# Seventeen groups of unread products between the norms and the wide layers of a kernel of two transformer blocks

## The chip, the cores and the metric

The kernel runs on one core of a Trainium2 chip. Its engines are TensorE (PE; matrix products into the PSUM banks), VectorE (DVE), ScalarE (ACT), GpSimd (POOL) and SyncE (SP, which here only issues loads). They run side by side and wait for each other through semaphores. The metric is the time of one execution on the device, in microseconds, as the median of several runs; less is better.

## The reference

Two blocks are computed for 512 tokens of width 1024. The first has two layers: one with a latent attention of 8 heads, which also carries 256 context tokens (768 together), and one with a gated linear attention of 4 heads; each is followed by a norm, a residual, a norm with modulation and an MLP with squared ReLU. The second has a gated delta rule of 8 heads and a retention of 4 heads, each followed by a layer norm, and by a convolutional feed-forward layer with another one. Cut to what matters here:

```
def rms_norm(x, g):
    y = x * rsqrt(mean(x * x, axis=-1) + NORM_EPS);  return y * g
h = modulate(rms_norm(x, norm_g[i, 0]), m[0], m[1])
y = mla_mixer(h, ...) if i == 0 else gla_mixer(h, ...)
x = x + m[2] * rms_norm(y, norm_g[i, 1])
h = modulate(rms_norm(x, norm_g[i, 2]), m[3], m[4])
x = x + m[5] * rms_norm(square(relu(h @ w1)) @ w2, norm_g[i, 3])
...
y = mixers[i](x * (1 + sc1) + sh1)             # delta rule, retention
x = layer_norm(ALPHA * x + (1 + g1) * y)
y = conv_ffn(x * (1 + sc2) + sh2)
x = layer_norm(ALPHA * x + (1 + g2) * y)
```

## The kernel before, in words

The residual stream lies transposed in `xT`: 8 blocks of 128 features by 768 or 512 tokens. A norm needs the sum of squares over features, that is, over partitions. ScalarE squares block after block into one of two buffers `sq` (L1301), and TensorE adds the blocks up by multiplying with a square of ones (`square_sum`, records L674 and L677, into the bank `sc[:, 0]`). When the last block is in, ScalarE takes a logarithm and an exponential (L1308, L1310, with a table load ahead of each), VectorE multiplies all blocks with the result (L1722 or L1738), adds the residual (L1742, L1743), and ScalarE modulates (L1325 to L1343). In all that time TensorE has nothing to do until the next squares or inputs come.

Wide products (output projections, MLPs, feed-forward layers, retention inputs) are computed from numbers split in two: a high part that ScalarE copies (`w_hi`, `x_hi`, `x_lo` as the high part of an output projection) and the rest, which VectorE subtracts (`w_lo`, `x_lo`, `attn_lo`, `g_out_lo`, `d_out_lo`, `wide_lo`; L1899, L1920, L1926, L1929). Three products of the halves stand for one; each leaves one record in the trace. All other f32 products leave two. In the first pass over an input TensorE waits for each of the 8 (or 16) blocks to be split; the later passes need no such wait.

Products go to the bank pairs `acc` and `sc`. The bank `sc[:, 1, 0]` takes scores, a projection and the sums of the linear attention at other times, and the bank beside it, `sc[:, 1, 1]`, collects the modulation (L735). `base_tab` holds an identity and the square of ones, side by side, 256 columns.

The order on each engine is that of the program text; an engine starts an instruction when its semaphores are there. No scheduler moves anything. The loops run over heads, quarters of the MLP width and column groups; the norms stand between them, outside of any loop.

Of the kernel before, what the change touches and what calls it, by code (L numbers as in the profile page):

```python
# [12 lines left out]
P = 128  # L13
# [10 lines left out]
GLA_H, GLA_DV, GATE_RANK = 4, 256, 16  # L24
# [110 lines left out]
def first_and_second_block(nc, A, out):  # L135
    ctx = ExitStack()
    with ctx:
        def sb(name, shape, dt=F32):
            return ctx.enter_context(nc.sbuf_tensor(name, shape, dt))

        def sem(name):
            return ctx.enter_context(nc.semaphore(name))
# [11 lines left out]
        base_tab = sb("base_tab", [P, 2 * P])  # L154
        ident, ones = base_tab[:, 0:P], base_tab[:, P:2 * P]
# [41 lines left out]
        sc = ctx.enter_context(nc.psum_tensor("sc", [P, 2, 2, 512], F32))  # L197
# [167 lines left out]
        gr_ready, gss_ready, gdev_ready = sem("gr_ready"), sem("gss_ready"), sem("gdev_ready")  # L365
# [73 lines left out]
        def emptied(eng, stage, it, j):  # L439

            u = UNIT0[stage] + j
            eng.wait_ge(acc_free[u % 2], u // 2 + 1 + it * (UNITS[stage] // 2))
# [190 lines left out]
        def _(pe):  # L633
# [32 lines left out]
            def square_sum(name, n, blocks=None):  # L666

                _, b0, nb = NORMS[name]
                for b in blocks or range(nb):
                    pe.wait_ge(n_sq, b0 + b + 1)  # L670
                    s = sq[:, (b0 + b) % 2]
                    if n == T:
                        for h in range(2):
                            last = pe.matmul(sc[:, 0, h, 0:HALF], ones, s[:, h * HALF:(h + 1) * HALF],  # L674
                                             start=b == 0, stop=b == nb - 1)
                    else:
                        last = pe.matmul(sc[:, 0, 0, 0:n], ones, s[:, 0:n], start=b == 0, stop=b == nb - 1)  # L677
                    last.then_inc(n_used, 1)

            def mean_sum(stage):  # L680

                for b in range(DB):
                    emptied(pe, stage, *divmod(b, UNITS[stage]))
                    last = pe.matmul(sc[:, 0, 1, :], ones, xT[:, b, CTX:T], start=b == 0, stop=b == DB - 1)  # L684
                last.then_inc(n_mean, 1)
# [65 lines left out]
            for h in range(2):  # L751
                last = pe.matmul(unit("mla_rope", 0)[:, h, 0:HALF], dup, kraw[0:64, h * HALF:(h + 1) * HALF],
                                 start=True, stop=True)
# [2 lines left out]
            pe.matmul(unit("mla_rope", 1)[:, 0, :], rotdup, kraw[0:64, CTX:T], start=True,  # L756
                      stop=True).then_inc(acc_ready, 1)
            square_sum("cq", T)
            square_sum("ckv", T)
            pe.wait_ge(lat_ready, 5)  # L760
            pe.wait_ge(krope_ready, 2)
            S = "mla_pair"
            columns = [None]
            with pe.Fori(0, MLA_H // 2) as it:
# [22 lines left out]
                for j in range(2):  # L787
                    claim(pe, S, it, 8 + j)
                    pe.matmul(unit(S, 8 + j)[:, 0, 0:256], rot2, qraw[:, CTX + 256 * j:CTX + 256 * (j + 1)],
                              start=True, stop=True).then_inc(acc_ready, 1)  # L790
# [49 lines left out]
            def second_half(stage, it, j):  # L840
                pe.wait_ge(w_split, half_group(stage, it, j, 1))
# [9 lines left out]
            def out_proj(stage, nk, per, squares=None):  # L851

                for j in range(8):
                    if squares and j > 2:
                        square_sum(*squares, [j - 3])
                    if j % per == 0:
                        w = split_group(stage, 0, j // per, nk, per * P)
                    claim(pe, stage, 0, j)
                    for k in range(nk):
                        if j == 0:  # L860
                            pe.wait_ge(o_split, OUT0[stage] + k + 1)
                        if j % per == 0 and k == nk // 2:
                            second_half(stage, 0, j // per)
                        last = split_product(unit(stage, j), w, (j % per) * P, k, out_parts(stage, k), k == 0, k == nk - 1)
                    last.then_inc(acc_ready, 1)
                if squares:
                    square_sum(*squares, range(5, 8))

            out_proj("mla_out", DB, 2, ("y0", T))

            def input_split(k, before):
# [3 lines left out]
            def mlp(i, n):  # L875
                S = f"mlp{i}"
                if n == T:
                    spans = [(h, HALF, slice(h * HALF, (h + 1) * HALF)) for h in range(2)]
                else:
                    spans = [(0, n, slice(0, n))]  # L880
                with pe.Fori(0, 4) as it:
                    for u in range(16):
                        if u % 2 == 0:
                            w = split_group(S, it, u // 2, DB, 256)
                        claim(pe, S, it, u)
                        for k in range(DB):
                            if u == 0:
                                input_split(k, DB * i)
                            if u % 2 == 0 and k == DB // 2:
                                second_half(S, it, u // 2)  # L890
                            if u == 8:
                                pe.wait_ge(relu_free, it * DB + (4 * DB * i + k + 3))
                            x = x_parts(n, k) if u < 8 else [(h, w_, hid_hi[:, k, t], hid_lo[:, k, t]) for h, w_, t in spans]
                            last = split_product(unit(S, u), w, (u % 2) * P, k, x, k == 0, k == DB - 1)
                        last.then_inc(acc_ready, 1)
                        if u in MOD_SUM_AFTER:
                            mod_sum(i, it, MOD_SUM_AFTER[u], 2 - i)

            square_sum("h0m", T)
            pe.wait_ge(mod_ready, 2)  # L900
            mlp(0, T)
            square_sum("y0m", T)


            square_sum("h1", T)
            pe.wait_ge(gate1_in, 16 * 2)
            for d in range(2):
                claim(pe, "gla_gate", 0, d)
# [4 lines left out]
            with pe.Fori(0, GLA_H) as it:  # L913
# [76 lines left out]
                for b in range(2):  # L990
                    last = pe.matmul(sc[:, 1, 0, :], ones, sq[:, b, 0:SEQ], start=b == 0, stop=b == 1)
                last.then_inc(gss_ready, 1)
            out_proj("gla_out", DB, 2, ("y1", SEQ))
            square_sum("h1m", SEQ)
            mlp(1, SEQ)
            square_sum("y1m", SEQ)


            pe.wait_ge(ab_in, 48)
# [18 lines left out]
            for r in range(2):  # L1018
                for c in range(LT):
# [5 lines left out]
                      stop=True).then_inc(d_cols, 1)  # L1025
# [131 lines left out]
            with pe.Fori(0, GDN_H // 2 - 1) as it:  # L1157
                gdn_pair(it, False)
            gdn_pair(GDN_H // 2 - 1, True)
            out_proj("gdn_out", DB, 2)  # L1160

            def ffn(i):
# [32 lines left out]

            mean_sum("gdn_out")
            square_sum("ln0", SEQ)
            ffn(0)
            mean_sum("ffn0_down")
            square_sum("ln0f", SEQ)  # L1200


            S = "ret_head"
            with pe.Fori(0, RET_H) as it:
# [62 lines left out]
                for b in range(4):  # L1267
                    pe.wait_ge(r_sq, it * 4 + b + 1)
                    last = pe.matmul(unit(S, 11)[:, 0, :], ones, r_sqr[:, b, :], start=b == 0, stop=b == 3)
                last.then_inc(acc_ready, 1)  # L1270
            out_proj("ret_out", 2 * DB, 1)
            mean_sum("ret_out")
            square_sum("ln1", SEQ)
            ffn(1)
            mean_sum("ffn1_down")
            square_sum("ln1f", SEQ)

            pe.wait_ge(x_ready, 64)
            for t in range(LT):
# [1203 lines left out]
```

## Time and profile before

| | us |
|---|---|
| median of 3 runs | 4133.73 (4129.1 to 4134.78) |
| the profiled execution, its own time | 4134.98 |
| its span, first to last instruction | 4133.3 |
| TensorE busy in it | 3758.0 (91%) |
| VectorE busy | 1793.3 (43%) |
| ScalarE busy | 1228.4 (30%) |
| mean granted clock of TensorE, as a share of full speed | 0.956 |

Times in the profile count from the start of the span. A record's duration is not its cost in a stream: products are pipelined, and their starts stand closer than they are long. What a product costs behind another is read from a stretch with many of them, divided by their number. The granted clock is 1.00 at 2.4 GHz and 0.50 at 1.2 GHz; a mean between them tells how much of a stretch lay at either level. The idle time in square brackets at the end of a row is that of the engine just ahead of the row, with the instruction that ended it.

### The profile page before, as it was taken

Reading aid. Unit: us, or ns where it says so; the run is one execution under the profiler, and the core shown is the slowest. Engines: PE = TensorE matmul, PEld = TensorE weight load, DVE = VectorE, ACT = ScalarE, POOL = GpSimd, SP = SyncE. Lnnn points to the kernel's source line nnn. Section 1 sums busy time; section 2 is a strip of 40 time slices with the busy share of each in tenths; the row PEclk is TensorE's granted clock in tenths of the full one; section 3 lists DMA queues with packets and bytes.
Section 4 is the critical chain, followed back from the end, with each engine's and each line's share of the span. In section 5 each row is a group of like instructions: output and inputs, shape, how many; then the busy total and the mean of one; then the engine's idle time right before and its main releaser. Section 6 shows DMA issues by size and latency. Waiting matters only on the chain.

```text
span 4133.3 us, 45599 instructions
## 1 busy us (share of the span) xinstructions
PE 3758.0 (91%) x17410; PEld 2905.1 (70%) x17410; DVE 1793.3 (43%) x2580; ACT 1228.4 (30%) x1511; POOL 155.9 (4%) x292
## 2 busy tenths in 40 slices
PE   6899997999998989799989999799977899899998
PEld 3477786999994656488856555668856677677876
DVE  1244445454444333455535544544444433435433
ACT  2111125132224222433323333244411322235432
POOL 0000000010000000011100000000022000000000
PEclk9999999999998999899999999899988999999999
DMA  4021112333220011144421011022255211122222
GB/s 153 31 83 62 62 54 69 103 120 100 94 91 31 31 36 36 57 164 165 162 90 31 31 41 33 18 79 91 91 167 171 87 61 61 61 82 88 95 86 76
DMA packets 300088, 335.15 MB, mean 81 GB/s; under 512 B 12113, under 2 KB 266449, under 8 KB 299857
## 3 DMA queue, kind: packets, MB, share of 16 engines
q1 hardware_dynamic: 271456, 250.69, 18.9%
q0 software_dynamic: 23040, 75.52, 5.5%
q10 hardware_dynamic: 5489, 7.47, 0.5%
q8 instruction: 76, 1.25, 0.1%
q14 instruction: 27, 0.22, 0.0%
HBM read 331.55 MB, written 2.10 MB: 81 GB/s over the span
## 4 chain that ended last, share of the span: by engine, by line
PE 83%; DVE 5%; ACT 4%; DMA 3%; issue 3%; ACTq 1%; DVEq 0%; POOLq 0%; POOL 0%; SPq 0%
PE acc L643 60%; PE sc L643 4%; PE sc L1086 2%; PE sc L674 2%; PE acc L823 1%; PE sc L797 1%; PE sc L799 1%; DMA rows_or_mod<-in_ada_w 1%; PE sc L735 1%; DMA rstd<-in_ada_w 1%; PE acc L1086 1%; PE sc L677 1%; PE acc L1256 1%; PE sc L684 1%; ACTq L1366 1%
## 5 line engine op out<-in xcount | busy, mean ns | idle before, releaser
L643 PE MATMUL acc<-x_lo,w_hi 128*128 128x512 f32 (+1 forms) x2048 | 775.8, 379 | 35.5 <-DVE d_out_lo L1899 10.5
L1417 ACT ACTIVATE w_hi<-wring 128x1024 fp32r<-128x1024 f32 (+1 forms) x368 | 352.0, 1004 | 1031.3 <-DMA wring<-in_mlp_w 479.6
L1920 DVE TENSOR_TENSOR w_lo<-wring,w_hi 128x1024 fp32r<-128x1024 f32 (+1 forms) x368 | 412.7, 1163 | 531.9 <-ACT w_hi L1417 531.7
L643 PEld LDWEIGHTS acc<-x_lo,w_hi 128*128 128x128 f32 x2048 | 388.8, 190 | 98.8 <-DVE w_lo L1920 28.4
L643 PE MATMUL acc<-hid_hi,w_hi 128*128 128x512 f32 (+1 forms) x1120 | 417.4, 373 | 5.1 <-DVE w_lo L1920 4.9
L643 PE MATMUL acc<-hid_hi,w_lo 128*128 128x512 f32 (+1 forms) x1120 | 413.0, 369 | 0.0
L643 PE MATMUL acc<-x_hi_holes,w_hi 128*128 128x512 f32 x704 | 279.1, 396 | 14.8 <-DVE x_lo L1926 14.8
L643 PE MATMUL acc<-x_hi_holes,w_lo 128*128 128x512 f32 x704 | 278.5, 396 | 0.0
L643 PE MATMUL acc<-hT,wring 128*128 128x512 f32 (+2 forms) x640 | 260.0, 567 | 14.1 <-DVE arena L1993 12.0
L643 PE MATMUL acc<-hid_lo,w_hi 128*128 128x384 f32 (+1 forms) x768 | 270.8, 353 | 0.0
L643 PE MATMUL acc<-x_hi_seq,w_hi 128*128 128x512 f32 x576 | 229.0, 398 | 14.4 <-DVE x_lo L1929 14.4
L643 PEld LDWEIGHTS acc<-hid_hi,w_hi 128*128 128x128 f32 x1120 | 214.5, 191 | 32.5 <-DVE w_lo L1920 6.9
L643 PEld LDWEIGHTS acc<-hid_hi,w_lo 128*128 128x128 f32 x1120 | 213.4, 191 | 25.3
L643 PEld LDWEIGHTS acc<-hT,wring 128*128 128x128 f32 (+1 forms) x640 | 124.8, 197 | 147.7 <-issue 97.0
L643 PE MATMUL acc<-x_hi_seq,w_lo 128*128 128x512 f32 x576 | 225.7, 392 | 0.0
L628 POOL DMA_DIRECT2D rows_or_mod<-in_ada_w x192 | 104.0, 542 | 2811.9 <-DVE hT L1722 1243.1
L643 PE MATMUL acc<-wide_lo,w_hi 128*128 128x512 f32 x480 | 192.6, 401 | 0.0
L1799 DVE SCALAR_TENSOR_TENSOR tab<-rows_or_mod,cs,tab 128x512 f32<-128x512 f32 x224 | 163.0, 748 | 61.6 <-DMA rows_or_mod<-in_ada_w 56.3
L643 PE MATMUL acc<-x_hi,w_hi 128*128 128x384 f32 x512 | 173.6, 339 | 13.5 <-DVE x_lo L1929 11.0
L643 PE MATMUL acc<-x_hi,w_lo 128*128 128x384 f32 x512 | 172.2, 336 | 2.1 <-issue 2.1
L643 PE MATMUL sc<-hT,wring 128*128 128x512 f32 x384 | 172.8, 595 | 0.4 <-DVE d_col L2100 0.4
L643 PEld LDWEIGHTS acc<-x_hi_holes,w_hi 128*128 128x128 f32 x704 | 133.0, 189 | 51.6 <-issue 14.8
(373 smaller groups left out, 5910.3 us busy)
## 6 DMA issues: line engine op xcount, KB each, us to landing
wring<-in_mlp_w SPq DMA_DIRECT2D x64, 1024.0 KB, 5.5
rows_or_mod<-in_ada_w POOLq DMA_DIRECT2D x192, 256.0 KB, 3.2
wring<-in_ffn_up SPq DMA_DIRECT2D x44, 1024.0 KB, 5.0
wring<-in_ada_w SPq DMA_DIRECT2D x12, 2048.0 KB, 7.8
rstd<-in_ada_w POOLq DMA_DIRECT2D x96, 256.0 KB, 3.2
wring<-in_ret_w_in SPq DMA_DIRECT2D x24, 1024.0 KB, 5.2
wring<-in_ffn_down SPq DMA_DIRECT2D x32, 704.0 KB, 4.6
wring<-in_gdn_w_in SPq DMA_DIRECT2D x16, 1024.0 KB, 5.7
```

What stands on the lines that cost most here:

```text
L628: pool.dma_start(mod_w[p % MOD_SLOTS], w[:, k, bass.ds(it * (MOD_IT * MOD_N) + i * MOD_N, MOD_N)]).then_inc(mod_loaded[p % MOD_SLOTS], 16)
L643: ins = pe.matmul(o, lhsT, rhs, start=start, stop=stop)
L674: last = pe.matmul(sc[:, 0, h, 0:HALF], ones, s[:, h * HALF:(h + 1) * HALF], start=b == 0, stop=b == nb - 1)
L677: last = pe.matmul(sc[:, 0, 0, 0:n], ones, s[:, 0:n], start=b == 0, stop=b == nb - 1)
L684: last = pe.matmul(sc[:, 0, 1, :], ones, xT[:, b, CTX:T], start=b == 0, stop=b == DB - 1)
L735: last = pe.matmul(mod_psum[:, bass.ds(it * (MOD_IT * per * nv) + c, 1)], mod_acc[:, i % 2, v, m * P:(m + 1) * P], ones[:, 0:1], start=Tru ...
L797: pe.matmul(sc[:, n % 2, h, 0:w], qn[:, e, t * P:(t + 1) * P], kn[:, e, k0:k0 + w], start=True, stop=False)
L799: last = pe.matmul(sc[:, n % 2, h, 0:w], qr[:, t * P:(t + 1) * P], krope[:, e, k0:k0 + w], start=False, stop=True)
L1086: last = pe.matmul(o[:, e, t], left[:, e, t], right[:, e, t], start=True, stop=True)
L1417: f(w_hi[s][:, c], wring[s][:, c], ACT.Copy).then_inc(w_high, 1)
L1799: ins = stt(a, mod_w[s], cs[:, k, v:v + 1], a, MUL, ADD)
L1920: tt(w_lo[s][:, c], wring[s][:, c], w_hi[s][:, c].bitcast(F32), SUB).then_inc(w_split, 1)
```

## The change

A new function on TensorE's side issues a number of products, 256 columns each, of the square of ones with the whole of `base_tab`, into `sc[:, 1, 0]`. Nothing reads that bank between such products and the next real product into it. The number is the argument divided by 0.43, rounded down. It is called at seventeen points of the program, all outside of loops; at one of them (ahead of the linear attention's output projection) a wait is added, for the last exponential of that attention, `gdev_ready`, because ScalarE has read a sum from this bank shortly before. No other engine's program is changed.

```
+            def keep_running(us):
+                for _ in range(int(us / 0.43)):
+                    pe.matmul(sc[:, 1, 0, 0:2 * P], ones, base_tab[:, :], start=True, stop=True)
...
             square_sum("cq", T)
+            keep_running(3)
             square_sum("ckv", T)
+            keep_running(6)
             pe.wait_ge(lat_ready, 5)
...
+            keep_running(6)
             out_proj("mla_out", DB, 2, ("y0", T))
...
+            keep_running(11.5)
             square_sum("h0m", T)
+            keep_running(6.5)
             pe.wait_ge(mod_ready, 2)
             mlp(0, T)
             square_sum("y0m", T)
+            keep_running(12.5)
             square_sum("h1", T)
+            keep_running(5)
             pe.wait_ge(gate1_in, 16 * 2)
...
+            pe.wait_ge(gdev_ready, GLA_H)
+            keep_running(7)
             out_proj("gla_out", DB, 2, ("y1", SEQ))
+            keep_running(8.5)
             square_sum("h1m", SEQ)
+            keep_running(5)
             mlp(1, SEQ)
             square_sum("y1m", SEQ)
+            keep_running(10)
             pe.wait_ge(ab_in, 48)
...
+            keep_running(9.5)
             out_proj("gdn_out", DB, 2)
...
             square_sum("ln0", SEQ)
+            keep_running(5)
             ffn(0)
             mean_sum("ffn0_down")
             square_sum("ln0f", SEQ)
+            keep_running(5)
...
+            keep_running(8)
             out_proj("ret_out", 2 * DB, 1)
             mean_sum("ret_out")
             square_sum("ln1", SEQ)
+            keep_running(5)
             ffn(1)
             mean_sum("ffn1_down")
             square_sum("ln1f", SEQ)
+            keep_running(8)
             pe.wait_ge(x_ready, 64)
```

TensorE's order ahead of the attention, before: sums of `cq` and `ckv` squares stand in one row, behind the key products.

```order
L643 MATMUL acc<-hT,wring 64x384 x16
L752 MATMUL acc<-arena,tab 128x384 x2
L756 MATMUL acc<-arena,tab 128x512
L674 MATMUL sc<-sq,base_tab 128x384 x10
L764 UNCONDITIONAL_BRANCH
```

The same place in the changed kernel, where the code's lines from L683 on are new or shifted (L674 is the sum, L683 the new product).

```order
L643 MATMUL acc<-hT,wring 64x384 x16
L757 MATMUL acc<-arena,tab 128x384 x2
L761 MATMUL acc<-arena,tab 128x512
L674 MATMUL sc<-sq,base_tab 128x384 x6
L683 MATMUL sc<-base_tab 128x256 x6
L674 MATMUL sc<-sq,base_tab 128x384 x4
L683 MATMUL sc<-base_tab 128x256 x13
L771 UNCONDITIONAL_BRANCH
```

Six products now stand between the two sums and thirteen behind the second; the sums themselves keep their order.

TensorE's order at the end of the linear attention with its waits, before: the last sum of squares (L991), the loop's end, and the output projection.

```order
L991 MATMUL sc<-sq,base_tab 128x512 [waits gsq_ready]
L991 MATMUL sc<-sq,base_tab 128x512
L913 REGISTER_ALU
L913 COMPARE_AND_BRANCH
L643 MATMUL acc<-x_lo,w_hi 128x512 [waits o_split,acc_free0,w_split]
L643 MATMUL acc<-g_out_lo,w_hi 128x512
```

The same place in the changed kernel.

```order
L1003 MATMUL sc<-sq,base_tab 128x512 [waits gsq_ready]
L1003 MATMUL sc<-sq,base_tab 128x512
L925 REGISTER_ALU
L925 COMPARE_AND_BRANCH
L683 MATMUL sc<-base_tab 128x256 [waits gdev_ready]
L683 MATMUL sc<-base_tab 128x256 x15
L643 MATMUL acc<-x_lo,w_hi 128x512 [waits o_split,acc_free0,w_split]
L643 MATMUL acc<-g_out_lo,w_hi 128x512
```

The new wait stands between the loop and the sixteen products; the projection keeps its own waits.

## Rows read from the trace of the kernel before

**Rows 1.** Page: busy share and instructions; clock in 40 slices; the chain by engine

```profile
PE 3758.0 (91%) x17410; PEld 2905.1 (70%) x17410; DVE 1793.3 (43%) x2580; ACT 1228.4 (30%) x1511; POOL 155.9 (4%) x292
...
PEclk9999999999998999899999999899988999999999
...
PE 83%; DVE 5%; ACT 4%; DMA 3%; issue 3%; ACTq 1%; DVEq 0%; POOLq 0%; POOL 0%; SPq 0%
```

**Rows 2.** Timeline, TensorE: start, us, engine, line, tiles, shapes, count [idle before <-releaser]

```profile
160.84 4.50 PE L674 MATMUL sc<-sq,base_tab 128*128 128x384 f32 x8 [3.88 <-ACT sq L1301]
...
651.07 12.88 PE L674 MATMUL sc<-sq,base_tab 128*128 128x384 f32 x32 [12.28 <-ACT sq L1301]
...
1239.23 10.48 PE L674 MATMUL sc<-sq,base_tab 128*128 128x384 f32 x32
1263.40 12.21 PE L674 MATMUL sc<-sq,base_tab 128*128 128x384 f32 x32 [13.69 <-ACT sq L1301]
1281.24 23.73 PE L643 MATMUL acc<-hT,gate 128*16 128x384 f32 x64 [5.63 <-ACT hT L1327]
```

**Rows 3.** Stretches behind restarts: us, busy PE PEld DVE ACT POOL, PEclk, DMA, GB/s

```profile
172.08:179.08 7.00, 7.00 (x13) 3.95 (x14) 0.00 (x0) 0.00 (x0) 0.00 (x0) 0.59 0.26 75
559.98:566.98 7.00, 7.00 (x31) 7.00 (x32) 5.93 (x7) 4.38 (x7) 0.00 (x0) 0.74 0.44 150
1669.13:1676.13 7.00, 7.00 (x23) 5.66 (x24) 4.07 (x7) 2.99 (x6) 0.00 (x0) 0.73 0.47 150
1731.22:1738.22 7.00, 7.00 (x12) 2.54 (x12) 6.20 (x7) 3.76 (x6) 0.00 (x0) 0.78 0.00 0
2129.84:2136.84 7.00, 7.00 (x12) 1.26 (x13) 3.59 (x6) 6.17 (x9) 0.00 (x0) 0.72 0.00 0
2676.71:2683.71 7.00, 7.00 (x24) 5.61 (x25) 4.06 (x8) 3.06 (x6) 0.00 (x0) 0.78 0.45 152
3615.51:3622.51 7.00, 7.00 (x25) 5.71 (x26) 7.00 (x13) 7.00 (x15) 0.00 (x0) 0.79 0.53 150
```

**Rows 4.** The same view, a stretch of 96 records of 256 columns and two neighbours

```profile
1329.70:1350.42 20.72, 20.72 (x98) 18.19 (x97) 11.67 (x23) 4.08 (x6) 0.00 (x0) 1.00 0.15 51
```

**Rows 5.** Timeline, TensorE: the first row behind nine other bubbles

```profile
172.08 7.30 PE L643 MATMUL acc<-arena,wring 128*128 128x384 f32 x13 [6.75 <-DVE arena L1833]
...
559.98 0.66 PE L643 MATMUL acc<-x_lo,w_hi 128*128 128x384 f32 x1 [6.42 <-DVE attn_lo L1899]
...
1669.13 0.77 PE L643 MATMUL acc<-x_lo,w_hi 128*128 128x512 f32 x1 [9.73 <-DVE g_out_lo L1899]
...
1731.22 1.22 PE L677 MATMUL sc<-sq,base_tab 128*128 128x512 f32 x1 [9.20 <-ACT sq L1301]
...
2129.84 15.79 PE L643 MATMUL acc<-hT,w_ab 128*8 128x512 f32 x32 [10.85 <-ACT hT L1336]
...
2676.71 0.76 PE L643 MATMUL acc<-x_lo,w_hi 128*128 128x512 f32 x1 [10.46 <-DVE d_out_lo L1899]
...
2744.86 0.76 PE L643 MATMUL acc<-x_hi_holes,w_hi 128*128 128x512 f32 x1 [5.93 <-DVE x_lo L1926]
...
3615.51 0.77 PE L643 MATMUL acc<-x_lo,w_hi 128*128 128x512 f32 x1 [8.85 <-DVE wide_lo L1899]
...
4122.69 0.69 PE L1283 MATMUL sc<-base_tab,xT 128*128 128x128 f32 x2 [9.33 <-ACT xT L1351]
```

**Rows 6.** Timeline, VectorE behind the sum at 651.07, and ScalarE ahead of 1669.13

```profile
667.07 1.83 DVE L1722 TENSOR_TENSOR hT<-xT,rstd 128x768 f32<-128x768 f32 x2 [0.90 <-ACT rstd L1310]
...
1661.44 0.63 ACT L1525 ACTIVATE rstd<-rstd 128x512 f32<-128x512 f32 x1
```

**Rows 7.** Stretches as in rows 3: two first passes of wide layers

```profile
676.20:685.87 9.67, 6.19 (x29) 4.58 (x29) 6.69 (x9) 9.54 (x15) 1.74 (x3) 1.00 0.31 106
2744.86:2754.35 9.49, 7.66 (x21) 4.26 (x21) 7.72 (x13) 9.28 (x14) 1.61 (x3) 0.83 0.48 159
```

**Rows 8.** Stretches as in rows 3: the last transposes and their four copies

```profile
4122.69:4130.04 7.35, 6.05 (x32) 5.56 (x32) 4.80 (x4) 0.00 (x0) 0.00 (x0) 0.70 0.39 156
```

More of the change, by code:

```diff
@@ L678, in square_sum, with keep_running @@
                     last.then_inc(n_used, 1)
+            def keep_running(us):
+                for _ in range(int(us / 0.43)):
+                    pe.matmul(sc[:, 1, 0, 0:2 * P], ones, base_tab[:, :], start=True, stop=True)
             def mean_sum(stage):
@@ L758, in _ @@
             square_sum("cq", T)
+            keep_running(3)
             square_sum("ckv", T)
+            keep_running(6)
             pe.wait_ge(lat_ready, 5)
@@ L867, in out_proj @@
                     square_sum(*squares, range(5, 8))
+            keep_running(6)
             out_proj("mla_out", DB, 2, ("y0", T))
@@ L897, in mlp @@
                             mod_sum(i, it, MOD_SUM_AFTER[u], 2 - i)
+            keep_running(11.5)
             square_sum("h0m", T)
+            keep_running(6.5)
             pe.wait_ge(mod_ready, 2)
@@ L902, in _ @@
             square_sum("y0m", T)
+            keep_running(12.5)
             square_sum("h1", T)
+            keep_running(5)
             pe.wait_ge(gate1_in, 16 * 2)
@@ L992, in _ @@
                 last.then_inc(gss_ready, 1)
+            pe.wait_ge(gdev_ready, GLA_H)
+            keep_running(7)
             out_proj("gla_out", DB, 2, ("y1", SEQ))
+            keep_running(8.5)
             square_sum("h1m", SEQ)
+            keep_running(5)
             mlp(1, SEQ)
             square_sum("y1m", SEQ)
+            keep_running(10)
             pe.wait_ge(ab_in, 48)
@@ L1159, in _ @@
             gdn_pair(GDN_H // 2 - 1, True)
+            keep_running(9.5)
             out_proj("gdn_out", DB, 2)
@@ L1197, in _ @@
             square_sum("ln0", SEQ)
+            keep_running(5)
             ffn(0)
@@ L1200, in _ @@
             square_sum("ln0f", SEQ)
+            keep_running(5)
             S = "ret_head"
@@ L1270, in _ @@
                 last.then_inc(acc_ready, 1)
+            keep_running(8)
             out_proj("ret_out", 2 * DB, 1)
@@ L1273, in _ @@
             square_sum("ln1", SEQ)
+            keep_running(5)
             ffn(1)
@@ L1276, in _ @@
             square_sum("ln1f", SEQ)
+            keep_running(8)
             pe.wait_ge(x_ready, 64)
```

## Prediction, before the changed kernel had run

> **What bounds the kernel now.** I read the page first. TensorE is busy 91% of the span and holds 83% of the chain that ended last, and the line of its granted clock is full nearly everywhere but dips to 8 in five of forty slices [rows 1]. So time is to be had where TensorE stands or runs at its lower level (1.2 instead of 2.4 GHz). Second, the timeline of TensorE around the places that the diff names: each row shows how long the engine stood, who let it go, and how long the work took that followed. Before the sum of squares at 1263.40 it stood 13.69 us, and the 32 records of that sum then took 12.21 us; the same 32 records at 1239.23, straight behind other products, took 10.48 [rows 2]. Third, the table by stretch: in the 7 us behind such an idle the granted clock averages 0.59 to 0.78 while TensorE is busy all 7 us [rows 3]. The kernel pays twice for a bubble: the bubble, which ScalarE and VectorE set, and slow products behind it.
>
> **What the change adds.** Seventeen calls issue 273 products (6, 13, 13, 26, 15, 29, 11, 16, 19, 11, 23, 22, 11, 11, 18, 11, 18), and one wait. Nothing is removed or moved. A plain f32 product leaves two records; 96 records of 256 columns follow each other in the 20.72 us of [rows 4] at full clock, 0.216 us each, so a product costs 0.432 us and all of them 118 us. They cost nothing as long as they end before the producer behind the next wait does. I check that bubble by bubble, product count times 0.432 against the idle: 2.6 of 3.88, 11.2 of 12.28, 12.5 of 13.69, 4.8 of 5.63 [rows 2]; 5.6 of 6.75, 5.6 of 6.42, 8.2 of 9.20, 9.9 of 10.85, 9.5 of 10.46, 7.8 of 8.85, 7.8 of 9.33, 4.8 of 5.93 [rows 5]. Four more calls stand in bubbles like the last one, ahead of the first pass of a wide layer. What is left of each bubble is 0.8 to 1.6 us, so I expect no late restart there, at full clock. The cover is the chain of logarithm, exponential, multiplications and splits on ScalarE and VectorE, which doesn't depend on these products: nobody reads the bank. If that chain were 1 us quicker in a bubble, its products would cost that excess.
>
> **What it gives, place by place.** If the clock stays at 2.4 GHz through the bubble, work that ran at half speed behind it takes half of that stretch. That is a gain only where TensorE itself then sets the pace.
> - Second norm of the attention (160.84): 8 records took 4.50 us; at 10.48/32 each they take 2.6. They follow each other without a break, so TensorE sets the pace: 1.8 us after rounding [rows 2].
> - First attention products (172.08), seven whole us at a clock of 0.59: 7 x 0.41 = 2.9 us. By the same product: the attention's output projection (559.98) 1.8, the sum at 1731.22 1.5, the gate products at 2129.84 2.0, the output projections at 2676.71 and 3615.51 1.5 each [rows 3]. In the projections VectorE has to keep ahead: at 559.98 a split takes 0.85 us (5.93 for 7), and 31 records in 7 - 1.8 us of full-clock work are 0.168 each, 1.0 for the six of a block; at 2676.71 it is 0.5 against 0.68 for three [rows 3]. So the products stay the slower side.
> - The sum at 1263.40: 12.21 - 10.48 = 1.7. The gate products at 1281.24: 64 records, 23.73 - 64 x 0.3275 = 2.8 us [rows 2].
> - The sum at 651.07: 12.88 - 10.48 = 2.4 on TensorE, but then VectorE starts the next multiplications at 667.07 after only 0.90 us of idle behind weight splits [rows 6]. VectorE is late next, so 0.9.
> - The linear attention's output projection (1669.13). Here the products wait for an exponential that ends at 1662.07 [rows 6], so that the bank has been read. Behind that wait stand only these products and the projection, whose own wait ends later. TensorE has then stood 2.7 us (since 1659.40), and 16 products end at 1669.0, with 0.1 us to spare. If the clock has fallen by then they overrun, by at most half of the slow stretches seen behind restarts (2.9 to 5.7 us, from 14 x (1 - clock)), so by up to 2.9. Full gain 7 x 0.27 = 1.9 [rows 3]; bounds -0.9 and 1.9. The idle lies between 3.88, behind which the products were slow, and the short pieces that left the clock full [rows 7]; it is near to neither, so I take the middle of the bounds, 0.5.
> - The last transposes (4122.69): 7.35 x 0.30 = 2.2 at most, but VectorE's four copies fill 4.80 of those 7.35 us and follow the first quarter of the transposes [rows 8]. I take 1.5.
> - The first passes of both MLPs, both convolution layers and the retention heads (five calls): nothing. There ScalarE is busy 9.54 of 9.67 and 9.28 of 9.49 us while TensorE waits for each block [rows 7]; when its last block comes, a full clock has only waited longer. For the same reason an overrun of a us or two costs nothing either.
>
> Sum: 1.8 + 2.9 + 1.8 + 1.5 + 2.0 + 3.0 + 1.7 + 2.8 + 0.9 + 0.5 + 1.5 = 20.4 us. The profiled execution took 4134.98 us, 1.7 more than its span, which the products don't touch; that gives 4114.6. The three timed runs had a median of 4133.73, 1.3 lower, which gives 4113.3. I forecast **4113 us**. How long the clock stays low behind a restart varies from place to place (2.9 to 5.7 us), and so does how often it falls in the loops that the change leaves alone; the three runs spread over 5.7 us.
>
> **Rivals.**
> *The clock falls anyway.* What is left of the bubbles, 0.8 to 1.6 us, may be enough to lose the clock, above all where the engine then works in pieces. Then the products buy nothing and the time is 4134, or 4130 with a few places won. Against it: between 676.20 and 685.87 TensorE was busy only 6.19 of 9.67 us, in pieces, and its clock was 1.00 throughout [rows 7]. The Trainium skill (TensorE: Matmul & The Clock Gate, section "A second HAM failure mode: psum-queue depth-cycling") says that frequent micro-idles between groups of matmuls make the clock swing between its levels. By that rule this rival would be the forecast; in this stretch the trace does not agree. I give it 9%.
> *Other engines set the restarts.* If the splits or squares, and not TensorE, pace the sums and projections as they do the first passes, only the attention's first products, the two gate products and the small norm pay in full: 2.9 + 2.0 + 2.8 + 1.8 = 9.5 us, with a little from the rest 12, so 4122. For it: it holds at five of seventeen places. Against it: in the sums TensorE's records leave no idle, and at full clock they took 10.48 without any. 12%.
> *The products are late (slower).* They are sized for 2.4 GHz. If a constant times ones doesn't keep the clock up, each takes 0.86 us and the bubble's products end long behind the producer. At the twelve places that pay (at the other five a late start is absorbed) they take 92 us at full clock; at half of it 92 us more, less some 12 us of slack, is 80 us: 4214. If the clock rises after at most 5.7 slow us, each loses at most 2.9, is 1.9 us late and then runs at full clock: 12 x 1.9 - 21 = +2, 4136. It is slower than 4142 from 2.4 us of lateness at each of the twelve. Against it: the sums multiply by the same ones and kept the clock for 10.48 us at 1239.23, and nearly all calls follow directly on such full-clock work [rows 2]. 4%.
> *The change doesn't do what it says.* If a product took half of 0.432 us, half of each bubble would stay empty and the clock fall; no gain, 4133. Against it are the 96 records of [rows 4]. 3%.
>
> **How the numbers follow.** Forecast 70%: 4113, give or take 6 for its bounds (the doubtful projection ±1.4, the transposes ±0.7, the varying slow stretches some ±3, the loops left alone ±3). Other engines 12%: 4122. Clock falls anyway 9%: 4132. Late products 4%: above 4142. No effect 3%: 4133. The rest, 2%, is more gain than summed, down to 4100. The range must reach the second case: 4104 to 4125. A measurement of this kernel can tell some 0.2%, 8.3 us, from no change: the bounds are 4125.5 and 4142. Faster: 70 + 12 + 2 = 84%, same 9 + 3 = 12%, slower 4%.
>
> **What would show it.** In the profile of the changed kernel each of the seventeen bubbles should hold the new line's records 0.216 us apart, with the idle before the restart down to 0.8 to 1.6 us (none at 1669). The granted clock behind the twelve paying restarts should be 1.00, and the sums of 32 records at 10.5 us. The first passes should end no earlier relative to their norm. The forecast is wrong if records stand 0.43 us apart, if restarts wait for no producer but for the products, if the clock behind them is still near 0.7, or if VectorE or ScalarE idles less than before yet TensorE's waits grow by as much as its products shrink.

## The result, and the profile of the changed kernel

The changed kernel took 4114.41 us (median of six runs, 4110.44 to 4116.82) beside 4134.18 for the kernel before (median of six): a ratio of 0.9950, 95% interval 0.9936 to 0.9964, some 20 us less. The forecast was 4113, range 4104 to 4125. The profiled execution took 4116.82 us with a span of 4115.1 (before: 4133.3).

The page, answering [rows 1]: busy share and instructions of each engine, the granted clock in 40 slices, the chain by engine.

```profile
PE 3852.5 (94%) x17956; PEld 2995.1 (73%) x17956; DVE 1792.6 (44%) x2580; ACT 1228.1 (30%) x1511; POOL 155.5 (4%) x292
...
PEclk9999999999999999999999999999988999999999
...
PE 82%; DVE 5%; ACT 4%; DMA 4%; issue 3%; ACTq 1%; DVEq 0%; POOLq 0%; POOL 0%; SPq 0%
```

TensorE is busy 94.5 us longer and yet ends 18 us earlier, since 118 us of products were added. VectorE, ScalarE and GpSimd do what they did. Three of the five dips in the line of the clock are gone; the two left lie in the second half of the first convolution layer, which the change leaves alone.

The timeline of TensorE at bubbles, answering [rows 2] and [rows 5] (line 683 is the new product; lines behind it have moved by up to 23):

```profile
152.64 2.75 PE L683 MATMUL sc<-base_tab 128*128 128x256 f32 x12
156.69 2.85 PE L674 MATMUL sc<-sq,base_tab 128*128 128x384 f32 x8 [1.29 <-ACT sq L1324]
159.37 5.78 PE L683 MATMUL sc<-base_tab 128*128 128x256 f32 x26
166.28 10.08 PE L643 MATMUL acc<-arena,wring 128*128 128x384 f32 x30 [1.14 <-DVE arena L1856]
...
632.79 11.39 PE L683 MATMUL sc<-base_tab 128*128 128x256 f32 x52
645.23 10.59 PE L674 MATMUL sc<-sq,base_tab 128*128 128x384 f32 x32 [1.06 <-ACT sq L1324]
...
1238.07 12.68 PE L683 MATMUL sc<-base_tab 128*128 128x256 f32 x58
1251.93 10.59 PE L674 MATMUL sc<-sq,base_tab 128*128 128x384 f32 x32 [1.18 <-ACT sq L1324]
...
1268.14 20.80 PE L643 MATMUL acc<-hT,gate 128*16 128x384 f32 x64 [0.88 <-ACT hT L1350]
...
1644.82 8.86 PE L683 MATMUL sc<-base_tab 128*128 128x256 f32 x32 [2.72 <-ACT rstd L1548]
1653.33 0.58 PE L643 MATMUL acc<-x_lo,w_hi 128*128 128x512 f32 x1
```

The 13.69 us ahead of the sum of 32 records [rows 2] are now 58 records in 12.68 us and 1.18 us of idle, and the sum takes 10.59 us instead of 12.21. Who lets TensorE go at these places is the same as before: results of ScalarE (squares, modulation) and of VectorE (splits above all). The one exception is the linear attention's output projection, which starts straight behind the last product, with no idle.

The same 7 us as in [rows 3] and the last transposes of [rows 8] (columns as there), for the attention's first products, the attention's output projection, the linear attention's, the sum that answers 1731.22, the gate products, the output projections of the gated delta rule and of the retention, and the last transposes:

```profile
166.28:173.28 7.00, 7.00 (x22) 4.22 (x23) 0.96 (x1) 0.00 (x0) 0.00 (x0) 1.00 0.24 75
555.81:562.81 7.00, 7.00 (x40) 7.00 (x41) 5.93 (x7) 3.41 (x5) 0.00 (x0) 1.00 0.47 152
1653.33:1660.33 7.00, 7.00 (x32) 5.80 (x31) 2.70 (x6) 1.70 (x3) 0.00 (x0) 1.00 0.45 150
1713.78:1720.78 7.00, 7.00 (x15) 2.46 (x16) 6.20 (x7) 4.85 (x8) 0.00 (x0) 1.00 0.00 0
2116.31:2123.31 7.00, 7.00 (x17) 1.51 (x18) 3.58 (x6) 6.17 (x9) 0.00 (x0) 1.00 0.00 0
2659.47:2666.47 7.00, 7.00 (x30) 5.71 (x31) 4.07 (x7) 2.86 (x5) 0.00 (x0) 1.00 0.46 152
3598.38:3605.38 7.00, 7.00 (x31) 5.82 (x32) 7.00 (x13) 7.00 (x15) 0.00 (x0) 1.00 0.53 150
4105.82:4110.45 4.63, 4.15 (x32) 3.43 (x32) 3.45 (x3) 0.00 (x0) 0.00 (x0) 1.00 0.31 123
```

The clock column reads 1.00 in every row (2.4 GHz) where it read 0.59 to 0.79, and the count of products in the 7 us has gone from 13 to 22, from 31 to 40, from 23 to 32. VectorE's busy time in the output projection at 555.81 is the same 5.93 us: the splits kept ahead.

### The profile page after: what moved, and what is told of

It reads as the page before. It is cut to its first block, busy times and chain, and to the rows that moved or that the text cites. A ratio compares the mean times of both kernels' runs of the same rounds, so it can differ in the third digit from the quotient of the medians.

```text
span 4115.1 us, 46691 instructions
## 1 busy us (share of the span) xinstructions
PE 3852.5 (94%) x17956; PEld 2995.1 (73%) x17956; DVE 1792.6 (44%) x2580; ACT 1228.1 (30%) x1511; POOL 155.5 (4%) x292
## 4 chain that ended last, share of the span: by engine, by line
PE 82%; DVE 5%; ACT 4%; DMA 4%; issue 3%; ACTq 1%; DVEq 0%; POOLq 0%; POOL 0%; SPq 0%
PE acc L643 59%; PE sc L643 4%; PE sc L1103 2%; PE acc L830 1%; PE sc L804 1%; PE sc L806 1%; PE sc L674 1%; DMA rows_or_mod<-in_ada_w 1%; PE sc L740 1%; DMA rstd<-in_ada_w 1%; PE acc L1103 1%; DMA wring<-in_mlp_w 1%; PE sc L677 1%; PE acc L1276 1%; PE sc L689 1%
## 5 line engine op out<-in xcount | busy, mean ns | idle before, releaser
L1943 DVE TENSOR_TENSOR w_lo<-wring,w_hi 128x1024 fp32r<-128x1024 f32 (+1 forms) x368 | 412.5, 1162 | 536.7 <-ACT w_hi L1440 536.7
```

The lines of the kernel that those rows point to most:

```text
L1943: tt(w_lo[s][:, c], wring[s][:, c], w_hi[s][:, c].bitcast(F32), SUB).then_inc(w_split, 1)
```

## The experiments

Theory: behind each bubble at which TensorE sets the pace, half of the stretch at the lower clock is won, and only there. Rivals: the gain has another source (a new layout of the program, other places); any work in the bubble would do; the five first passes pay as well. The runs below were made in three sets; a kernel's ratio is to the kernel before in its own set.

**The twelve paying calls alone.** Of the seventeen, the five calls ahead of first passes go:

```diff
-            keep_running(6.5)
             pe.wait_ge(mod_ready, 2)
             mlp(0, T)
...
-            keep_running(5)
             mlp(1, SEQ)
```

and the same ahead of `ffn(0)`, the retention heads and `ffn(1)`.

> The five calls ahead of the first passes of the two MLPs, the two convolution layers and the retention heads are left out, the other twelve stay. Theory (a full clock pays only where TensorE sets the pace): the five give nothing, so the time stays at that of the whole change, 4114 us, give or take 3, and the first passes end as long behind their norm as with the calls. Rival (a fuller clock pays at every restart): each of the five was worth 1 to 2 us like the others, so 4119 to 4124.

Measured: 4117.24 us, ratio to before 0.9948 (0.9932 to 0.9963); the whole change in the same set of runs 4115.4, 0.9944 (0.9929 to 0.9959). The 2 us between them can't be told from nothing, but not surely from the rival's 5 either; the trace decides. In the first convolution layer's first pass, which runs over the 8 blocks that VectorE splits, the timeline of TensorE shows the first and the last block's restart, and the table by stretch the pass between them (columns as in [rows 3]). Without the call:

```profile
2726.52 0.77 PE L643 MATMUL acc<-x_hi_holes,w_hi 128*128 128x512 f32 x1 [5.93 <-DVE x_lo L1944]
...
2736.01 0.50 PE L643 MATMUL acc<-x_hi_holes,w_hi 128*128 128x512 f32 x1 [0.39 <-DVE x_lo L1944]
```

```profile
2726.52:2736.01 9.49, 8.22 (x22) 4.74 (x22) 7.72 (x13) 9.28 (x14) 1.61 (x3) 0.74 0.50 154
```

In the changed kernel, with it:

```profile
2726.19 0.47 PE L643 MATMUL acc<-x_hi_holes,w_hi 128*128 128x512 f32 x1 [1.18 <-DVE x_lo L1949]
...
2735.68 0.50 PE L643 MATMUL acc<-x_hi_holes,w_hi 128*128 128x512 f32 x1 [0.41 <-DVE x_lo L1949]
```

```profile
2726.19:2735.68 9.49, 6.68 (x21) 3.37 (x21) 7.72 (x13) 9.28 (x14) 1.61 (x3) 1.00 0.50 159
```

The pass takes 9.49 us at a clock of 0.74 as at 1.00: VectorE's splits set it. At the second MLP, the retention heads and the second convolution layer it is the same, with 0.59 to 0.79 without the call and 1.00 with it in the first 7 us. The first MLP can say nothing on a full clock. Its bubble is longer, its call left 2.32 us of idle, and the clock fell in spite of it:

```profile
664.61:671.61 7.00, 6.31 (x21) 5.39 (x22) 6.20 (x7) 6.87 (x11) 0.00 (x0) 0.58 0.49 150
```

So four calls are worth nothing because another engine sets the pace, and the fifth did not keep the clock.

**The same instructions, with nothing in them.**

```diff
-                    pe.matmul(sc[:, 1, 0, 0:2 * P], ones, base_tab[:, :], start=True, stop=True)
+                    pe.matmul(sc[:, 1, 0, 0:2], ones, base_tab[:, 0:2], start=True, stop=True)
```

> All 17 calls stay with their 273 products, but each product has 2 columns instead of 256, so that the bubbles are nearly as empty as before while the program holds the same instructions. Theory (the gain is the clock, held by the streaming of columns): the clock falls as before and the time is that of before, 4134 us, give or take 4; the twelve restarts show a granted clock of 0.6 to 0.8 in the 7 us behind them. Rival (the gain is another layout of the instructions: with the change the five or six idles of 0.5 to 1 us at the loop turns of the first MLP, 4.6 us in all, were gone): those idles are gone here too, 4129. Rival (any product keeps the clock up): 4114, clock 1.00 behind the restarts.

Measured: 4136.73 us, 0.9994 (0.9986 to 1.0003): no gain that these runs can tell. The changed kernel, which has the same instructions with 256 columns each, took 4115.4 us in the same set, 21 us less, so the gain doesn't come from the layout of the program. The timeline ahead of the sum of 32 records, and the table by stretch for part of that bubble, of this kernel:

```profile
1244.77 9.44 PE L683 MATMUL sc<-base_tab 128*128 128x2 f32 x56
1258.48 11.99 PE L674 MATMUL sc<-sq,base_tab 128*128 128x384 f32 x32 [4.28 <-ACT sq L1324]
```

```profile
1247.70:1254.20 6.50, 6.50 (x31) 6.42 (x31) 4.87 (x6) 1.51 (x2) 0.00 (x0) 0.50 0.25 81
```

TensorE counts as busy for all of these 6.5 us, and the granted clock is 0.50 all the same: busy time in the table does not tell whether the clock will hold. The idles at the loop turns of the first MLP were gone here too: it took 561.6 us from its first products to the next sum of squares, instead of 567.8 and 567.4 in the two profiles of the kernel before. So that rival holds for those idles, 6 us in the trace (in the time of the whole 2 us show, with an interval from 6 less to 1 more), but not for the 21 us.

**Half the products.** The divisor in `keep_running` is doubled, so the second half of each bubble stays empty.

```diff
-                for _ in range(int(us / 0.43)):
+                for _ in range(int(us / 0.86)):
```

> Each of the 17 calls issues half of its products (132 in all), so the second half of each bubble is empty: idles of about 2.6 us ahead of the attention's second norm, 3.3 to 4.2 us at the gate products of the linear attention and in the attention, and 5 to 7.5 us at most others. Theory (what counts is how long TensorE stands just ahead of the restart; in the kernel before a restart behind 3.88 us was slow already): most restarts are slow again, two or three are not, 4129 us (4124 to 4134). Rival (some work inside the bubble is enough, wherever it stands): the clock stays full, 4114 us.

Measured: 4133.58 us, 0.9988 (0.9976 to 1.0000). Of the twelve places eleven were slow again (0.59 to 0.80 in the 7 us behind the restart), the shortest behind 2.59 us of idle, so nearly all the gain was gone; two or three were expected to hold. The one that held is the linear attention's output projection. Its timeline here:

```profile
1657.00 5.41 PE L683 MATMUL sc<-base_tab 128*128 128x256 f32 x16 [2.72 <-ACT rstd L1548]
1664.01 0.47 PE L643 MATMUL acc<-x_lo,w_hi 128*128 128x512 f32 x1 [1.61 <-DVE g_out_lo L1922]
```

Eight products, run partly at the lower clock, ended 1.6 us ahead of the restart, and from the sum of squares to the end of that projection it took 60.88 us; the whole change, with 16 late products, took 62.48, and the kernel before 62.62.

**One and a half times the products.**

```diff
-                for _ in range(int(us / 0.43)):
+                for _ in range(int(1.5 * us / 0.43)):
```

> All 17 calls with one and a half times their products (409 instead of 273). Theory (at the twelve paying places TensorE sets the pace, and what a call overruns comes onto the time; at the five first passes it is absorbed): half of each call's length less the idle that the changed kernel has left there, 0 + 1.7 + 2.0 + 4.5 + 5.0 + 1.5 + 3.5 + 3.1 + 4.0 + 3.8 + 2.8 + 2.3 = 34 us, so 4148 us (4143 to 4155), with a full clock behind all restarts. Rival (the restarts are set by other engines, the gain has come from elsewhere): 4114 to 4125.

Measured: 4149.3 us, 1.0033 (1.0020 to 1.0046), 35 us above the changed kernel (34 to 37 by the ratios of the two sets) for 34 summed. At none of the seventeen places does the restart now wait for a producer, as here around the sum of 32 records:

```profile
1252.11 18.73 PE L683 MATMUL sc<-base_tab 128*128 128x256 f32 x86
1270.67 10.48 PE L674 MATMUL sc<-sq,base_tab 128*128 128x384 f32 x32
1280.99 7.50 PE L683 MATMUL sc<-base_tab 128*128 128x256 f32 x34
```

So the length is what the gain hangs on in both directions: short and the clock is lost, long and the excess is paid in full.

**The doubtful projection, with the wait removed.** Another bank needs no wait for the exponential:

```diff
-            pe.wait_ge(gdev_ready, GLA_H)
-            keep_running(7)
+            keep_running(9, 1)
...
-                    pe.matmul(sc[:, 1, 0, 0:2 * P], ones, base_tab[:, :], start=True, stop=True)
+                    pe.matmul(sc[:, 1, h, 0:2 * P], ones, base_tab[:, :], start=True, stop=True)
```

> Ahead of the linear attention's output projection the products go into the other bank of the same pair, so that they need no wait for the exponential, and there are 20 of them instead of 16. Theory (there the clock fell in the idle ahead of the products, 16 of them then ran late and ate the gain): they now follow the last head's sum directly, the clock stays full, about 1 us of idle is left, and this place gives 1.6 us more: 4112.8 us, a step that only the trace can tell from 4114.4. Rival (the projection is paced by its splits there): the same time as the whole change, with more idle inside the projection.

```profile
1638.13 8.88 PE L683 MATMUL sc<-base_tab 128*128 128x256 f32 x40
1648.08 0.47 PE L643 MATMUL acc<-x_lo,w_hi 128*128 128x512 f32 x1 [1.06 <-DVE g_out_lo L1921]
```

From the sum to the projection's end 60.86 us instead of 62.48: 1.62 won, as expected. The time, 4115.98 us (0.9947, 0.9935 to 0.9959), can't show so little.

**The two kernels once more,** unaltered.

> The changed kernel once more, unaltered, for a second profile: 4114 us, give or take 3. If the idles at the loop turns of the first MLP are a matter of the program, they are absent again, and the waits of the second MLP for late weight splits (4.4 us in the first profile) are there again; if they are a matter of the single execution, one of the two differs.

> The kernel before, unaltered, for a second profile: 4134 us (4128 to 4140). If the idles of 0.5 to 1 us at the loop turns of the first MLP and the lack of late weight splits in the second MLP are a matter of the program, both are here again as in its first profile; if they are a matter of the single execution, one of the two differs.

Measured: 4115.4 and 4137.65 us. Waits of TensorE in the first MLP's loop (line, what it waited for: us in total, times, longest), kernel before, first and second profile:

```profile
PE acc L643 <- issue: 4.6, 6, 1.1
```

```profile
PE acc L643 <- issue: 4.1, 6, 1.0
```

Neither profile of the changed kernel has such a row: a matter of the program. In the second MLP it is the other way. The first profile of before had none of the waits below, the second has them, and so has the changed kernel; first before (second profile), then changed:

```profile
PE acc L643 <- DVE arena L1955: 3.7, 3, 2.1
```

```profile
PE acc L643 <- DVE arena L1978: 4.4, 5, 2.1
```

From that MLP's start to the gate products behind it, it took 383.5 us in the first profile of before, 388.4 in the second, 388.9 in the changed kernel and 387.0 to 392.6 in the nine others. That this place seemed to lose 5.4 us was the luck of one execution of the kernel before.

**Into the loops.** What is left at the lower clock lies in loops. The first version put 3 products ahead of each sum and 7 behind the gate products of a linear-attention head, 8 between the two sums of squares of a delta-rule pair, 2 at the scores of an attention pair.

```diff
+                keep_running(1.3, 1)
                 pe.wait_ge(gsq_ready, it * 1 + 1)
...
+                    if j == 2:
+                        pe.wait_ge(qk_moved, it * 2 + 2)
+                        keep_running(3.5, 1)
                     pe.wait_ge(d_sq, it * 3 + n)
```

> The version before this one, and such products also inside three loops: 2 ahead of the first scores of each pair of attention heads, 3 ahead of the sum and 7 behind the gate products of each head of the linear attention, 8 between the two sums of squares of each pair of heads of the gated delta rule. Theory (a clock that fell in a bubble costs half of its low stretch wherever TensorE sets the pace): per head of the linear attention 10 us at the lower clock go, 5 us gained, times 5, less an overrun or two; per pair of the gated delta rule up to 17 us of it, 8 us gained in two of four; per pair of attention heads 1.7; together 25 to 40 us, so 4082 us (4072 to 4095). Rival (inside the loops VectorE and ScalarE set the pace, as at the five first passes): 4113 us, with the idles longer by what the products save.

Measured: 4103.13 us, 0.9923 (0.9910 to 0.9935): some 11 us less than the changed kernel, where 25 to 40 were expected: outside the stated range, and not the rival's 4113 either. A head of the linear attention and two pairs of the delta rule, changed kernel and then this one (columns as in [rows 3]):

```profile
1464.15:1553.17 89.02, 80.50 (x316) 53.60 (x315) 30.38 (x47) 24.11 (x29) 0.00 (x0) 0.92 0.11 36
2302.06:2554.70 252.64, 233.96 (x1113) 150.95 (x1112) 129.51 (x225) 79.67 (x96) 0.00 (x0) 0.95 0.11 33
```

```profile
1464.22:1550.60 86.38, 83.07 (x336) 57.31 (x335) 30.39 (x47) 24.11 (x29) 0.00 (x0) 0.96 0.12 37
2295.12:2542.68 247.56, 234.73 (x1144) 155.18 (x1145) 129.50 (x225) 79.42 (x97) 0.00 (x0) 0.98 0.12 34
```

A head gained 2.6 us where 5 were expected, a pair 2.5. The clock still fell twice in that head. The first fall lay on the 7 products behind the gate products, and so they took 4.98 us instead of some 3.0 (14 records at 0.216) and ended late, with no idle behind them:

```profile
1466.99 4.98 PE L683 MATMUL sc<-base_tab 128*128 128x256 f32 x14
```

The second, from 1522.1 to 1525.6, lay among the state products. In the attention's loop I had put the products behind the wait and not ahead of it: they filled nothing, and that part tells nothing.

The second version has none there, 8 products at the end of a head instead of 7 behind the next one's gate products, and 3 and 1 more among the state products.

```diff
+                        if (d, i) in ((0, 4), (1, 0)):
+                            keep_running(1.3 if d == 0 else 0.43, 1)
...
                 last.then_inc(gss_ready, 1)
+                keep_running(3.5, 1)
```

> The version with products inside the loops, rearranged after its trace: none in the attention's loop, where the first version gained nothing; per head of the linear attention 8 behind the sum of squares (ahead of the next head's gate products, and not behind them, so that the first head has none), 3 ahead of that sum and 3 and 1 ahead of the two later groups of state products, where the clock fell; per pair of the gated delta rule 2 and 8 ahead of the two sums. In the first version a head took 87.2 and 86.4 us instead of 89.1, a pair 123.4 instead of 125.6. Theory (the clock that is left low in those loops still costs TensorE half of its stretch where it sets the pace): heads of 85 to 86 us and pairs of 122 to 123, 4098 us (4090 to 4104). Rival (other engines set what is left): 4103 us as the first version, its idles longer instead.

Measured: 4093.61 us, 0.9895 (0.9880 to 0.9910), faster than both kernels, about 20 us below the changed one. The same stretches:

```profile
1454.92:1540.72 85.80, 83.61 (x345) 57.47 (x344) 30.37 (x49) 24.11 (x29) 0.00 (x0) 0.98 0.12 37
2281.62:2527.52 245.90, 234.78 (x1153) 156.31 (x1153) 129.47 (x225) 79.43 (x97) 0.00 (x0) 0.99 0.12 34
```

The whole loop of heads took 370.6 us from the gate products to the output projection, after 385.2 in the changed kernel and 379.1 in the first version; the delta rule 534.6 after 543.2 and 536.7.

**Where another engine sets the pace.** In the first convolution layer's second half TensorE waits for the modulation:

```diff
+                                if j == 0:
+                                    keep_running(5.2)
                                 mod_sum(2, it, DOWN_SUM_AFTER[j, k], 1)
...
+                            keep_running(5.2)
                             mod_sum(2, it, 2, 1)
```

> The whole change, and 12 products (5.2 us) ahead of each of the eight sums of the modulation in the first convolution layer's second half at which TensorE stands 5.8 to 9.7 us, and behind which its clock is low for some 10 us. Theory (there VectorE's chain of modulation products sets when TensorE goes on, 64.6 us of waits in all; a full clock behind such a sum only lengthens the next wait): no gain, 4114 us (4109 to 4118), waits on VectorE at those sums longer in total than the 64.6 us less the products. Rival (TensorE sets the pace behind each restart): 8 stretches of 10 us at half speed, 5 us each, 40 us less: 4075 us.

Measured: 4109.32 us, 0.9928 (0.9908 to 0.9949), which can't be told from the changed kernel; the 40 us of the rival are excluded. Waits of TensorE there, changed kernel and then this one:

```profile
PE sc L740 <- DVE tab L1822: 64.6, 8, 9.7
```

```profile
PE sc L740 <- DVE tab L1825: 23.8, 8, 4.2
```

The stretch's clock, from the first of those waits to the layer's end:

```profile
2984.96:3206.42 221.46, 156.81 (x607) 123.79 (x607) 100.15 (x146) 22.62 (x30) 50.34 (x93) 0.81 0.52 161
```

```profile
2982.59:3199.30 216.71, 192.10 (x799) 154.88 (x799) 100.42 (x146) 22.63 (x30) 50.22 (x93) 0.91 0.53 164
```

Waits plus products (8 times 5.2) are 65.3 us, as before 64.6: the products went into the waits. The clock rose from 0.81 to 0.91, and the stretch became 4.7 us shorter in this trace, not the 22 (0.10 of 221) that it would give if TensorE set its length. The 4.7 us are more than the spread between executions, since the same stretch took 219.9 to 222.4 us in the eleven other profiles. So most of the products' effect went into the waits, as the theory has it, but its "no gain" was off by some 3 to 5 us.

## Why the prediction was right

**The places.** What each gave, as the growth of the distance between the two traces (before and changed kernel, first profiles) across the place, beside the forecast:

| Place | gave, us | forecast |
|---|---|---|
| second norm of the attention | 1.66 | 1.8 |
| first attention products | 2.84 | 2.9 |
| attention's output projection | 1.68 | 1.8 |
| sum answering 651.07, up to the MLP's start | 0.99 | 0.9 |
| sum answering 1263.40 | 1.63 | 1.7 |
| gate products, linear attention | 2.93 | 2.8 |
| linear attention's output projection | 0.14 | 0.5 |
| sum answering 1731.22 | 1.51 | 1.5 |
| gate products, delta rule | 1.9 | 2.0 |
| output projections, delta rule and retention | 1.43 + 1.40 | 3.0 |
| last transposes | 1.45 | 1.5 |
| four of the five first passes | 0 | 0 |
| first pass of the first MLP | -1.5 | 0 |

The twelve paying places give 19.6 together for 20.4. The forecasts were read from the same profile of the kernel before. Against its second profile they also give 20, but single places differ by up to 1.6: the gate products of the linear attention give 1.4 there, those of the delta rule 2.9. So the total is firmer than its terms. What was read off ahead held at eleven paying places: half of the stretch at the lower clock, 0.8 to 1.6 us of idle left, VectorE as the next limit at the MLP's start. There the sum itself became 2.29 us shorter (10.59 instead of 12.88) and the MLP started only 0.99 earlier relative to it; the rest stands as idle.

**The one term that was mis-sized** is the linear attention's output projection, 0.14 for 0.5 of bounds -0.9 and 1.9. Both halves of its mechanism are in the trace: behind the 2.72 us of idle the products began at a clock of 1.00, which fell to 0.50 from 1645.4 to 1648.8, so that they took 8.86 us instead of 6.9 and the restart came 11.23 us behind the sum instead of 9.73, and the projection then ran 1.65 us shorter at full clock. The run with another bank and the run with half the products show that the late part can be had back.

**One reading was loose:** "Four more calls stand in bubbles like the last one" is wrong for the first MLP. Its bubble was 7.5 us, and the 1.3 us that the sum ahead of it gained without the MLP starting earlier made it 8.8, for 6.5 us of products; the prediction had counted that rest as lost, but not as idle here. So 2.3 us were left and the clock fell. The call could save nothing by it: the pass took as long without it (665.12 to 679.55 from the first block to the last, 664.61 to 679.03 with it). In the first profile of the changed kernel the clock fell once more, at 679.4, when the last block had come and TensorE set the pace; that is the 1.5 us in the table. The run without the five calls shows the same fall, the second profile of the changed kernel does not.

**The rivals.** *The clock falls anyway* fell at the paying places: 1.00 behind eleven of eleven idles of 0.8 to 1.6 us, while in the run with half the products idles from 2.6 us up lost it. It came true in the first MLP's first pass, where the engine works in pieces: in the changed kernel the clock was low from 665.8 to 672.6 and from 679.4 to 682.8, with idles of 0.7 to 0.8 us between. So the row of the same pass at 1.00 [rows 7], on which the prediction leant against this rival, did not carry over. The Trainium skill (TensorE: Matmul & The Clock Gate, section "A second HAM failure mode: psum-queue depth-cycling") ties swings of the clock to frequent micro-idles; the fall at 679.4 agrees. No such swing shows behind the paying restarts, nor in the four other first passes, whose idles were 0.3 to 0.5 us. *Other engines set the restarts* holds for the first passes, as forecast; the run without their calls shows it at four of the five. *The products are late* was put to the test by longer ones, and its price (half of each call less the idle left) came out as 35 us for 34 summed. *It doesn't do what it says* fell with 52 records in 11.39 us.

**What the sum left out** has terms as large as a quarter of it, and came out nearly even: the two spans differ by 18.2 us where the places gave 19.6. The first MLP gave 4.6: some 6 from the idles at its loop turns, which had nothing to do with the clock, less the 1.5 of its first pass. The start gave 4.2, the loops of the linear attention and the delta rule 1.3 and 1.8 (in the first, the last sum itself became 1.7 us slower, because a fall of the clock now lay on it). The attention's loop took 4.5 (7 falls of the clock in it instead of 3), the second MLP 5.4, the two convolution layers 1.6 each. The repeated profiles place the first MLP's idles in the program, and the second MLP, the start and the attention's loop in the execution (in the second profile of the changed kernel the start gave nothing, the attention's loop 1.7); which falls in the loops come with a given execution was not settled. So the forecast's error of 1 us is partly luck; the 6 us that it allowed itself were nearer to what it could know. The comparison that is free of the idles, with the kernel of 2 columns, gives 21 us for 20.4.

## What to carry to other kernels

Products that nobody reads are worth issuing where three things hold: the engine stands long enough to lose the clock, it sets the pace behind the restart, and they fit the bubble (0.8 to 1.6 us left kept the clock at eleven places, 2.3 lost it at one). Read each of the three from the trace of that place, not from shares of the whole: here twelve of seventeen places paid, 1.6 us on average, one of them next to nothing. A loop pays per turn, so look there next, and put the products ahead of the wait, in a bank that needs no wait of its own.

## What the runs showed of the hardware that was not expected

**The clock fell while the engine was busy.** In the run with 2 columns, TensorE followed one record with the next from 1244.63 to 1254.20 without idle, and from 1247.70 on the granted clock was 0.50 (the row is with that run); with 58 records of 256 columns in the same place it was 1.00 throughout.

**Instructions added in one place removed idles in another.** The kernel before stands 4.1 and 4.6 us in two profiles, in six pieces of up to 1.1 us, at the loop turns of the first MLP. With the 273 products, full or of two columns, there are none; without the five calls, or with half or one and a half times the products, three pieces and 2.5 to 2.8 us. The queue that carries instructions went along: kind, packets, megabytes and share of the page, before and changed kernel.

```profile
q8 instruction: 76, 1.25, 0.1%
```

```profile
q8 instruction: 53, 0.87, 0.1%
```

It had 78 to 82 packets in the three kernels with three idles, and 53 in all seven profiles with none. The Trainium skill (Runtime: NRT & Kernel Launch, section "Instruction fetch mechanics") says that a taken branch whose target lies outside the pages at hand has to wait for them to be fetched; idles at loop turns that come and go with the number of packets agree, but where the loop lies in memory was not varied by itself. In the time as a whole it can't be seen: 0.9948 with 79 packets, 0.9944 with 53.
